# The state update of a chunked recurrence on VectorE: old state times the end factors ahead of the chain, then one product with a scalar and an added tensor per direction

## The reference, cut to what matters

```python
def wkv7_scan(s0, r, w, kk, a, k, v):
    def step(s, inp):
        r_t, w_t, kk_t, a_t, k_t, v_t = inp
        s_kk = jnp.einsum('bhvk,bhk->bhv', s, kk_t)
        s = (s * w_t[:, :, None, :] - s_kk[..., None] * (kk_t * a_t)[:, :, None, :]
             + v_t[..., None] * k_t[:, :, None, :])
        return s, jnp.einsum('bhvk,bhk->bhv', s, r_t)
    ...
```

## Time and profile before

| | |
|---|---|
| median of 3 runs | 3311.26 us (3309.19 to 3319.1) |
| profiled execution: time | 3302.93 us |
| profiled execution: span of the core | 3301.3 us |
| granted TensorE clock, mean | 0.942 of full |
| busy: TensorE, VectorE, ScalarE, GpSimd | 87%, 59%, 42%, 16% |
| stage `pairs`, steady part | 96 us for a pair of heads |

### The profile page before, as it was taken

How to read it: one execution, slowest core, us unless ns; L and a number is a source line. 1 busy time by engine, 2 the same in 40 slices (tenths; PEclk the granted TensorE clock), 3 DMA queues, 4 the chain that set the end, 5 groups by cost and what they waited for, 6 DMA issues and landing times. The chain is left out here.

```text
span 3301.3 us, 70036 instructions
## 1 busy us (share of the span) xinstructions
PE 2858.2 (87%) x30245; PEld 2351.2 (71%) x30245; DVE 1932.0 (59%) x3065; ACT 1372.7 (42%) x2028; POOL 536.4 (16%) x489
## 2 busy tenths in 40 slices
PE   7998799989989569999735999999965987769999
PEld 2564678788778448887515999999963754548877
DVE  5431455666565345765663888888875146456652
ACT  2002445444444322212213777777753345333331
POOL 3001445454344110000001000000010025100000
PEclk9999899999999789999966999999987999889999
DMA  4643000000000128664306999999951210122322
GB/s 193 220 153 104 6 20 20 20 20 20 20 3 4 65 87 309 268 252 172 112 15 260 365 371 363 372 371 362 371 207 61 99 53 18 51 78 90 102 101 78
DMA packets 74015, 483.10 MB, mean 146 GB/s; under 512 B 11123, under 2 KB 13043, under 8 KB 32288
## 3 DMA queue, kind: packets, MB, share of 16 engines
q1 hardware_dynamic: 59360, 418.48, 34.0%
q0 software_dynamic: 12096, 52.43, 4.3%
q10 hardware_dynamic: 2304, 8.39, 0.6%
HBM read 457.73 MB, written 34.13 MB: 149 GB/s over the span
## 5 line engine op out<-in xcount | busy, mean ns | idle before, releaser
L2156 DVE TENSOR_TENSOR sb_moe_w_lo<-w_ring,sb_moe_w_hi 128x1408 fp32r<-128x1408 f32 (+1 forms) x132 | 255.2, 1934 | 67.7 <-ACT sb_moe_w_hi L2110 67.5
L2056 PE MATMUL ps<-sb_moe_w_hi,sb_x_feat_lo 128*128 128x352 f32 x832 | 274.3, 330 | 11.5 <-DVE sb_moe_w_lo L2156 11.5
L2058 PE MATMUL ps<-sb_moe_w_hi,sb_x_feat_hi 128*128 128x352 f32 x832 | 268.4, 323 | 0.0
L2057 PE MATMUL ps<-sb_moe_w_lo,sb_x_feat_hi 128*128 128x352 f32 x832 | 267.8, 322 | 0.0
L2110 ACT ACTIVATE sb_moe_w_hi<-w_ring 128x2816 fp32r<-128x2816 f32 x80 | 204.1, 2553 | 0.1
L2056 PEld LDWEIGHTS ps<-sb_moe_w_hi,sb_x_feat_lo 128*128 128x128 f32 x832 | 157.0, 189 | 17.3 <-issue 17.0
L2056 PE MATMUL ps<-sb_moe_w_hi,sb_hid_feat_lo 128*128 128x256 f32 x572 | 163.3, 285 | 3.9 <-DVE sb_hid_feat_lo L2182 3.9
L2058 PE MATMUL ps<-sb_moe_w_hi,sb_hid_feat_hi 128*128 128x256 f32 x572 | 161.9, 283 | 0.0
L2057 PE MATMUL ps<-sb_moe_w_lo,sb_hid_feat_hi 128*128 128x256 f32 x572 | 161.9, 283 | 0.0
L1321 DVE STREAM_TRANSPOSE sb_tb<-sb_tb 128x128 f32<-128x128 f32 x384 | 106.0, 298 | 93.6 <-ACT sb_tb L1230 91.5
L231 PE MATMUL ps<-sb_ffn_features,sb_hi_ffn 128*128 128x512 f32 x352 | 140.2, 398 | 22.1 <-DVE sb_lo_ffn L219 22.1
(11 more groups left out here) (511 smaller groups left out, 7924.3 us busy)
## 6 DMA issues: line engine op xcount, KB each, us to landing
w_ring<-w_moe_up SPq DMA_DIRECT2D x67, 1408.0 KB, 8.3
sb_hm<-w_ada SPq DMA_DIRECT2D x48, 1024.0 KB, 6.9
w_ring<-w_ffn SPq DMA_DIRECT2D x22, 1024.0 KB, 4.8
w_ring<-w_up SPq DMA_DIRECT2D x22, 1024.0 KB, 4.9
sb_t_again<-w_moe_up SPq DMA_DIRECT2D x13, 1408.0 KB, 8.5
sb_hm<-w_moe_up SPq DMA_DIRECT2D x13, 1408.0 KB, 8.3
sb_b_again<-w_moe_up SPq DMA_DIRECT2D x13, 1408.0 KB, 7.9
w_ring<-w_moe_down SPq DMA_DIRECT2D x13, 1408.0 KB, 7.6
```

The costliest lines, as they stand in the source:

```text
L2056: pe.matmul(out, x_lo, w_hi, start=first, stop=False)
L2057: pe.matmul(out, x_hi, w_lo, start=False, stop=False)
L2058: return pe.matmul(out, x_hi, w_hi, start=False, stop=end)
L2156: return V.tensor_tensor(WL[:, s, w], raw[raw_at(c, i)[0]][:, w], WH[:, s, w].bitcast(F32), ALU.subtract)
```

## The change

The new state is computed as increment times end factor, plus old state times end factor. The second part needs nothing of the current step, and is computed at the place of `U{n}` in VectorE's order, by two instructions (one per direction, 64 columns) which multiply by a scalar of each partition and add a tile of zeros, `nil`. At the place of `Z{n}` two more instructions, again one per direction, multiply the increment in PSUM by the scalar and add that product. The semaphore value `sum{n}` is replaced by `ends{n}`.

```diff
-        dve_c = self.marks("chain_dve", [y for x in links if x[0] == "Z" for y in ([f"sum{x[1:]}"] if x != "Z0" else []) + [f"z{x[1:]}"]])
+        dve_c = self.marks("chain_dve", [y for x in links if x[0] == "Z" for y in ([f"ends{x[1:]}"] if x != "Z0" else []) + [f"z{x[1:]}"]])
...
+            nil, s_nil = self.sb(st, "nil", CH), self.sem("nil_set")
...
+                    V.memset(nil[:, :], 0.0).then_inc(s_nil, 1)
+                    dve.wait_ge(s_nil, 1)
...
+                        elif head == "U" and 0 < n < NCH - 1:
+                            dve.wait_ge(dve_c.sem, dve_c.at(f"z{n - 1}", p))
+                            for d in range(2):
+                                c = chunk_at(n, d) // CH
+                                last = V.scalar_tensor_tensor(out=Zs[:, d, :], in0=Zb[:, n % 2, d, :], scalar=PE2[:, u, d, c:c + 1],
+                                                              in1=nil[:, 0:CH], op0=ALU.mult, op1=ALU.add)
+                            last.then_inc(*dve_c.did(f"ends{n}"))
                         elif head == "Z":
                             dve.wait_ge(pe_c.sem, pe_c.at(x, p))
-                            b = ps[:, 5, 3 * P:4 * P].rearrange("p (d n) -> p d n", d=2)
                             if n:
-                                V.tensor_tensor(Zs[:, :, :], b, Zb[:, n % 2, :, :], ALU.add).then_inc(*dve_c.did(f"sum{n}"))
-                                dve.wait_ge(dve_c.sem, dve_c.at(f"sum{n}", p))
-                                b = Zs[:, :, :]
-                            end = PE2[:, u, 0, chunk_at(n, 0) // CH:chunk_at(n, 0) // CH + 1]
-                            step = NCH + (chunk_at(n, 1) - chunk_at(n, 0)) // CH
-                            last = V.tensor_tensor(Zb[:, (n + 1) % 2, :, :], b,
-                                                   AP(end.tensor, end.offset, [end.ap[0], (step, 2), (0, CH)]), ALU.mult)
+                                dve.wait_ge(dve_c.sem, dve_c.at(f"ends{n}", p))
+                            for d in range(2):
+                                c = chunk_at(n, d) // CH
+                                last = V.scalar_tensor_tensor(out=Zb[:, (n + 1) % 2, d, :], in0=ps[:, 5, 3 * P + d * CH:3 * P + (d + 1) * CH],
+                                                              scalar=PE2[:, u, d, c:c + 1], in1=Zs[:, d, :] if n else nil[:, 0:CH],
+                                                              op0=ALU.mult, op1=ALU.add)
                             last.then_inc(*dve_c.did(f"z{n}"))
```

## The result

| | before | after |
|---|---|---|
| median of 6 runs | 3310.23 us | 3334.27 us (3324.97 to 3336.07) |
| span of the profiled execution | 3301.3 us | 3323.4 us |

The ratio is 1.0063, with a 95% interval of 1.0048 to 1.0079: slower by 24 us, where 45 were forecast. It lies in the stated range, and the sign is right, but the size is off by nearly a factor of two.

What follows compares the result with a forecast made beforehand. TensorE was taken to set the pace, busy 86.8 of 96 us a pair. Turns with GpSimd 38 us, plus first steps 10, minus stretch given back 3, made 45: 3311.3 + 45 = 3356 us, range 3304 to 3390.

Steps and rivals of the forecast that it cites:

- The mechanism at step 4: In the chain's step 4, a whole GpSimd operation (L872) runs between the two early products; state at 716.0, against 714.83 before.
- the walk: Pair 3 followed through steps 4 to 7 with VectorE and GpSimd taking turns: 5.5 us later a pair.
- Rival A: At the early products, no turn-taking: the second follows the first at once, so faster, 3300 us; chance 0.13.
- C: State products on the chain collide with GpSimd too, four instructions a step taking turns: 77 us more, 3388 us; chance 0.14.
- B: Turns are taken, but fewer later collisions and the crowded first steps swallow the loss: no difference, about 3311 us; chance 0.13.
- the crowded first steps: First steps of a pair, VectorE busy 4.53 of 4.60 us: added instructions cost 1.2 us a pair, 10 us in all.
- 5.5 us a pair, 38 us for seven: Delay from early products taking turns with GpSimd's long run, once in each of seven pairs; bounds 31 and 45 us.
- the sum: Whole change: 38 us of turns, plus 10 for first steps, minus 3 of old stretch given back: 45 us slower.
- L882 goes between: At step 6, GpSimd's L882 runs between the two early products; product two ends at 727.3, state at 728.5, before 723.10.
- the lower bound: If in step 6 product one comes just ahead of L879: 4.5 us a pair, 31 us in all.
- Seven alike: GpSimd's long run comes once for each pair with a next one, so pair 3's 5.5 us was taken seven times.
- TensorE's wait: TensorE's waiting in the stage moves from 35 us to some 70, at U and at the masks' followers.

## Why the prediction was right or wrong

**Right.** The mechanism at step 4: a GpSimd operation between the two early products (5.77 us for the two; the walk had 5.8, from 709.0 to 714.82), and state products that stay at 0.27 and are never stretched. A middle pair of 102.3 us where about 102 was said is luck, as shown below. Rival A is refuted by step 4 of six pairs, where the second product takes 3.45 us or more, and C by the maximum of 0.286. B named one thing rightly: the crowded first steps cost little.

**The step that failed** is "5.5 us a pair, 38 us for seven". The seven pairs grew by 19.1 us together, from the start of one step 0 to the next, and this holds the first steps as well, for which the sum had 10 us more. One move of the walk was wrong even in its own case: at step 6, "L882 goes between". The ends of the states in a middle pair, counted from the start of step 0's state (681.89 in the kernel before, 579.22 after), follow. The rows are those of step 0 and step 8, before and then after:

```profile
681.89 0.25 DVE L1335 TENSOR_TENSOR sb_Z<-ps,sb_pend 128x128 f32<-128x128 f32 x1
```
```profile
746.41 0.29 DVE L1335 TENSOR_TENSOR sb_Z<-sb_Z_sum,sb_pend 128x128 f32<-128x128 f32 x1
```

```profile
579.22 0.42 DVE L1342 SCALAR_TENSOR_TENSOR sb_Z<-ps,sb_pend,sb_nil 128x64 f32<-128x64 f32 x2
```
```profile
649.73 0.48 DVE L1342 SCALAR_TENSOR_TENSOR sb_Z<-ps,sb_pend,sb_Z_sum 128x64 f32<-128x64 f32 x2 [0.91 <-PE ps L1120]
```

| end of the state of step | 4 | 5 | 6 | 7 | 8 |
|---|---|---|---|---|---|
| before, us from step 0 | 32.9 | 36.5 | 41.2 | 44.8 | 64.8 |
| after | 33.0 | 36.6 | 42.2 | 48.0 | 71.0 |
| difference | 0.1 | 0.1 | 1.0 | 3.2 | 6.2 |
| the walk | 1.2 | 1.2 | 5.4 | 5.5 | |

GpSimd's first two long operations beside the first pair, in the kernel before:

```profile
390.16 3.44 POOL L869 TENSOR_TENSOR sb_sg<-sb_a,sb_kk 128x1536 f32<-128x1536 f32 x1 [6.56 <-DVE sb_kk L1272]
...
411.58 3.44 POOL L872 TENSOR_TENSOR sb_ex<-sb_ex,sb_kk 128x1536 f32<-128x1536 f32 x1
```

- *Within the pair* the walk was 2.3 us too long at step 7. It took the masks of step 4 to end where they did before, and they end 0.8 us earlier; and in step 6 product one came just ahead of L880, the case that stood in the text as the lower bound (4.5 us). The fourth pair is the walk's own case, product one behind the start of L880, and there L883, the L882 of the kernel before, did not go between the two products (720.75 to 724.23, above). The prediction had said that GpSimd goes next where it has work queued, and did not ask whether L882 was ready while L879 ran. With this put right the walk comes to 4.3 us at step 7 (an estimate: product two at 724.1, step 6's state at 725.3, product one of step 7 at 727.4 behind L882, product two at 729.8 behind L888, the state at 731.0); measured in that pair are 4.5.
- *That the pair took 102.3 us all the same* comes from what the walk did not have: 3.0 us more between steps 7 and 8, where the clock was granted at 0.50 for 3.4 us twice. The sum has no term for the clock. The pair's figure was right by two errors that cancel, which is luck.
- *Seven alike* was the larger error. Five pairs, the third to the seventh, grew, by 4.3 to 6.6 us from step 0 to step 0. The first pair became 7.4 us shorter. There GpSimd's long operations do not all come one behind the other in steps 4 to 7: in the kernel before, the first runs at step 1 and the second starts 18 us after its end (the two rows above). Its old multiplications were stretched up to 2.85 us, and it had the half clock from 393.3 on for 6.8 us and in two more pieces; after, the clock is 1.00 throughout. The second pair became 1.3 us shorter, and the last one, which has no features beside it, 3.0 us from its step 0 to its last state; its two stretched multiplications (1.22 and 1.39 us) are gone. Over all pairs, from the first state to the last, the stage grew by 16.1 us (725.5 to 741.6), where the sum had 45.
- *The crowded first steps* were 10 us in the sum; the run with early products there alone gives 2 to 5 us. Against the kernel before, the changed one is even 0.5 us ahead in a middle pair when the state of step 3 ends (13.9 against 14.4).
- *TensorE's wait* at U was to go to 70 us; it stayed at 35.9, and the masks' took 9 more. So these two waits hold 9.4 of the 16.1 us by which the stage grew.

**What is shown and what stays open.** Shown: the change is 59 us of early products against 35 us gained on the chain. Most of the 59 comes from waits for single GpSimd operations: on ScalarE, where nothing waits for GpSimd, 44 of them are gone; operations in halves take 22 to 27 off; one multiplication in the place of two takes 47 off. Not shown is why a GpSimd operation that has to wait for its own predecessor misses its turn; that it does is seen at step 6 in ten cases (two pairs of the changed kernel, seven with four products, one without the zeros), with no case against it, but always at the same operation, L883. How much is the clock is only estimated: the kernel before has two kinds of middle pairs, 96.1 us and, with 3.4 us at half speed, 98.0, so 0.56 us lost per slow us; by the trace's record of the clock the stage has 20.5 slow us before and 34.1 after, so some 8 of the 22 us by which the spans differ. The rate is rough: with four products the stage has 121 slow us more, which at 0.56 would be 68 us, more than the whole rise. No kernel here changed the clock alone. Of the 22 us, 2 lie ahead of the first state and 4 behind the last, in stages that the change does not touch. The part behind the last state takes 2187 to 2194 us over the twelve traces, in no order with the change, so these 4 us are scatter between executions.

## What to carry to other kernels

Before moving work ahead of a chain, look at what the moved instruction reads and what runs on GpSimd at that place. A VectorE instruction held up by GpSimd pays by the instruction, not by its size, so one of 128 columns is better than two of 64 (3287 against 3334 us), and long GpSimd operations in portions shorten each wait. The kernel with as much stretch behind the masks, with TensorE's work still queued, was 23 us faster than the one with it between the two links of the chain. When counting turns, ask of each operation of the other engine whether it is ready or still waits for its own predecessor. A pattern read from one period should be checked against the first and the last before it is multiplied, above all where a race of 0.2 us decides, as at step 6.

## What the runs showed of the hardware that was not expected

- A multiplication by a scalar of each partition, one 64-column fp32 tile of SBUF to another (0.246 us in the median), is held up by GpSimd as well, up to 3.527 us. So one SBUF input is no protection. State updates with PSUM as the source were never held up in any run (maxima of 0.285 to 0.293 us).
- In these runs the two engines took turns only where the next GpSimd operation was ready. Behind L880, two products (3.28 and 0.27 us, the fourth pair of the changed kernel) or two of four (3.4 and 0.24 us, six pairs) went through before L883, which waits for L880.
- TensorE was granted its lower clock, 1.2 GHz (0.50), for 3.4 us twice in each of four middle pairs of the changed kernel. Ahead of the first such piece of the third pair it was busy 11.4 of 16.2 us, ahead of the second 11.6 of 13.7. With four products a step the pieces were 3.4, 6.8 and 10.2 us long. That the pauses are the cause is not shown: the kernel before has a piece in one middle pair too, and the kernel with the early products on ScalarE has one in each of six pairs, though its stage is 35 us shorter.
